# Moving row factors of a pooling stage from VectorE to GpSimd, and splitting its first residual pair by chunk

## The chip, the cores and the metric

The kernel runs on one NeuronCore of a Trainium2 chip. Its engines are named as the profile names them: PE is TensorE (PEld its weight loads), DVE is VectorE, ACT is ScalarE, POOL is GpSimd, and SP issues the transfers. The metric is the device time of one execution in microseconds (us); less is better.

## The reference

A stack of layers over 256 frames of 1024 channels. The stretch that matters is the hand-over from the first block to the second: a final norm, then a second norm, a pooling mixer with a residual sum, and the gated feed-forward stage after it.

```
h = h + ffn(...)                      # end of the first block (stage F1)
x = rms_norm(h, norm_final)
h = rmsnorm(x, mix_norm[0])
pooled_g = trailing mean of h over (2, 4, 8, 16) frames, group g of 256 channels
y = (pooled - h) @ pool_w[g] + pool_b
x = x + y * pool_scale                # stage POOL
x = x + conv_ffn_2(rmsnorm(x, ffn_norm[0]), ...)   # stage F2
```

## The kernel before

The activations lie transposed in SBUF: `xT` (inside the tensor `gx`) holds 8 chunks of 128 channels, each 128 partitions by 256 frames in float32. Each matmul runs on numbers that are split in a high part and a low part. ACT makes the high part (`split_x` in the scalar program, L1209, a copy with a gain into `xx`, which counts up the semaphore `s_xh`), and DVE the low part (`split_x` in the vector program, L1742, gain times `xT` less the high part, which counts up `s_xl`). The weights come as units that ACT and DVE split in the same way (L1206, L1737). Every engine runs a program written out by hand, in the order of the code, and the engines meet only at semaphores.

Stage POOL has four groups of 256 channels, two chunks each. PE multiplies the split chunks with the pool weights (L433 to L435) while the sums of squares of the last chunks come in. DVE makes the row factors from the sums: a chain of 12 tiny instructions (L2285 to L1777) gives `ra`, one number per frame. ACT scales the products with it into `zz` (L1644). DVE also multiplies `ra` into a diagonal, `dg` (L1812), PE spreads it over all partitions (L535, L536), and DVE copies that to `rb` (L1817), which counts up `s_rb`. PE then applies the averaging windows to `zz`, 16 pairs of short matmuls (L1172, L1174), and counts up `s_zw` for each group. ACT adds bias and scale to the results, `pu` (L1651, chunk by chunk, `average(k)`), and counts up `s_uu` after the second chunk of a group.

DVE has to bring `xT` through the final norm, `xT * norm_final * rb` (`normed`, L2298, one instruction for each of the 8 chunks), and then adds `pu` for each pair of chunks (`averages(g)`, L2305), which counts up `s_res`. ACT and DVE split the new chunks for stage F2, ACT squares them for the next norm (L1215, L1221), and DVE adds the squares up (L1750). In F2 PE takes the gate unit for chunks 0 and 1, then the value unit for chunks 0 and 1, and from chunk 2 on gate and value for one chunk after the other (L474, L476). Each chunk takes four pairs of matmuls of its own and waits for `s_xh` and `s_xl` of that chunk (`x_here`).

GpSimd has nothing to do up to the last attention stage, where it sets parts of the tiles `bm` (L2366, L2367). The sums that F2 needs for its own norm go through `fold_sums` and `low_sums` (L1793, L1798).

Of the kernel before, what the change touches and what calls it, by code (L numbers as in the profile page):

```python
# [10 lines left out]
ALU = mybir.AluOpType  # L11
# [3 lines left out]
S, D, KD = 256, 1024, 8  # L15
# [26 lines left out]
A, F0, B, F1, POOL, F2, DD, F3 = range(8)  # L42
# [59 lines left out]
def build(nc, dram, out):  # L102
    plan, first = unit_plan()
    N_UNITS = len(plan)
    with ExitStack() as ctx:
        def sb(name, shape, dt=F32, stack=ctx):
            return stack.enter_context(nc.sbuf_tensor(name, shape, dt))
# [5 lines left out]
        def sem(name):  # L113
            return ctx.enter_context(nc.semaphore(name))
# [5 lines left out]
        s_con, s_vec, s_win, s_bias, s_out, s_sin = (  # L120
            sem(f"s_{x}") for x in ("con", "vec", "win", "bias", "out", "sin"))
# [5 lines left out]
        s_xh, s_xl, s_res = sem("s_xh"), sem("s_xl"), sem("s_res")  # L127
# [3 lines left out]
        s_dg, s_row, s_rb, s_ones = sem("s_dg"), sem("s_row"), sem("s_rb"), sem("s_ones")  # L131
# [18 lines left out]
            sem(f"s_{x}") for x in ("kr", "krr", "krt", "qr", "rope", "qrt", "qre"))  # L150

        s_pp, s_zz, s_zw, s_gg, s_uu = (sem(f"s_{x}") for x in ("pp", "zz", "zw", "gg", "uu"))

        s_dv, s_ac = sem("s_dv"), sem("s_ac")

# [4 lines left out]
        xT = gx[:, KD:].rearrange("p (k s) -> p k s", k=KD)  # L160
# [52 lines left out]
        pu = sb("pu", [128, KD, S], F32, pool_mem)  # L213
# [11 lines left out]
        def vcol(name, i):  # L225
            return vec[:, VEC_AT[name] + i:VEC_AT[name] + i + 1]
# [11 lines left out]
        rbb = rb[:, :].unsqueeze(1).to_broadcast([128, 2, S])  # L238
# [5 lines left out]
        def bk(s, i):  # L244


            return bank[(2 * FLIP[s] + i) % 4]
# [56 lines left out]
        def n_x(s, k):  # L304

            return 8 * s + k + 1

        def n_res(s, c):

            return 4 * s + c + 1  # L310
# [7 lines left out]
        ROW = {F0: 1, F1: 2, POOL: 3, F2: 4, F3: 5}  # L318
# [872 lines left out]
        def scalar_program(e):  # L1191
# [16 lines left out]
            def split_x(s, k):  # L1208
                e.activation(xx[:, k, 0, :], xT[:, k, :], ACT.Copy, scale=gain_of(s, k)).then_inc(s_xh, 1)  # L1209
# [423 lines left out]
            def pool_mixer():  # L1633
                s = POOL
                u = first[s]
                e.wait_ge(s_rc, COL[s])
                for g in range(NG):
                    b = bk(s, g)
                    if g < 3:
                        e.wait_ge(s_pp, g + 1)  # L1640
                    else:
                        e.wait_ge(s_used, u + 1)
                    for h in range(2):
                        last = e.activation(zz[:, h, g * 256:(g + 1) * 256], b[:, h * 256:(h + 1) * 256], ACT.Copy,  # L1644
                                            scale=ra[:, 2 + h:3 + h])
                    last.then_inc(s_zz, 1)

                def average(k):
                    g, m = k // 2, k % 2
                    e.wait_ge(s_zw, g + 1)  # L1650
                    done = e.activation(pu[:, k, :], bk(s, g)[:, m * 256:(m + 1) * 256], ACT.Identity,  # L1651
                                        scale=vcol("pool_scale", k), bias=bs[:, k:k + 1])
                    if m == 1:
                        done.then_inc(s_uu, 1)

                def averages(g):
                    average(2 * g)
                    average(2 * g + 1)

                def split_pair(g):  # L1660
                    e.wait_ge(s_res, n_res(s, g))
                    split_x(F2, 2 * g)
                    split_x(F2, 2 * g + 1)

                averages(0)
                average(2)
                split_pair(0)
                average(3)
                squares(F2, 0)
                split_pair(1)  # L1670
                averages(2)
                squares(F2, 1)
                split_pair(2)
                averages(3)
                squares(F2, 2)
                split_pair(3)
                squares(F2, 3)
                high_sums(F2)
                hi(u + 5)
# [41 lines left out]
        def vector_program(e):  # L1721
# [7 lines left out]
            def after_own():  # L1729
                e.wait_ge(s_dv, own["n"])  # L1730
# [549 lines left out]
            def pool_mixer():  # L2280
                s = POOL
                u = first[s]
                e.wait_ge(s_sum, s + 1)
                sums = SB[:, 0, 0:4].rearrange("p (h w) -> p h w", h=2)
                e.tensor_scalar(va[:, 0:2], sums[:, :, 0], 1.0 / D, EPS, ALU.mult, ALU.add)  # L2285
                kept(e.tensor_scalar(va[:, 2:4], sums[:, :, 1], 1.0 / D, None, ALU.mult))
                after_own()
                kept(e.scalar_tensor_tensor(out=va[:, 2:4], in0=va[:, 0:2], scalar=EPS, in1=va[:, 2:4], op0=ALU.mult,
                                            op1=ALU.add))
                rsqrt(va, ra, ta).then_inc(s_rc, 1)  # L2290
                norm_diag(s, ra)
                norm_row(s, 0)
                e.wait_ge(s_rb, ROW[s])
                e.wait_ge(s_xh, n_x(s, KD - 1))

                def normed(*chunks):
                    for k in chunks:
                        kept(e.scalar_tensor_tensor(out=xT[:, k, :], in0=xT[:, k, :], scalar=vcol("norm_final", k),  # L2298
                                                    in1=rb[:, :], op0=ALU.mult, op1=ALU.mult))

                def averages(g):
                    xp = xT[:, 2 * g:2 * g + 2, :]
                    e.wait_ge(s_uu, g + 1)
                    after_own()
                    e.tensor_tensor(xp, xp, pu[:, 2 * g:2 * g + 2, :], ALU.add).then_inc(s_res, 1)  # L2305

                normed(0, 1, 2)
                averages(0)
                normed(3)
                split_x(F2, 0)  # L2310
                split_x(F2, 1)
                averages(1)
                normed(4, 5)
                split_x(F2, 2)
                split_x(F2, 3)
                normed(6, 7)
                averages(2)
                add_squares(F2, 1)
                split_x(F2, 4)
                split_x(F2, 5)  # L2320
                averages(3)
                add_squares(F2, 2)
                split_x(F2, 6)
                split_x(F2, 7)
                lo(u + 3)
                add_squares(F2, 3)
                fold_sums(F2)
                low_sums(F2)
                lo(u + 4)
# [31 lines left out]


        def gpsimd_program(e):
            e.wait_ge(s_used, first[DD])
            for b in bm:
                e.memset(b[0:64, :, 64:128], -1e30)  # L2366
                last = e.memset(b[0:64, :, 320:384], -1e30)  # L2367
            last.then_inc(s_bm, 1)
# [15 lines left out]
        @block.gpsimd  # L2384
        def _(e):
            gpsimd_program(e)
# [130 lines left out]
```

## Time and profile before

| what | value |
|---|---|
| median of 3 runs | 1062.54 us (1062.38 to 1062.83) |
| time of the profiled execution | 1062.58 us |
| its span in the trace | 1060.8 us |
| PE busy | 1056.1 us, 6764 matmuls |
| DVE busy | 835.5 us |
| ACT busy | 649.2 us |
| POOL busy | 1.3 us |
| granted PE clock in the stretch from 575 to 600 us | 1.00 (the 2.4 GHz level) |

The time of the profiled execution has 1.78 us beside its span. The span counts from the first to the last recorded event. Busy time of an engine is the time in which an instruction of it is on record; matmuls overlap, so PE starts the next one before the record of the last has ended, and the distance between starts is what PE needs for one. In a row of a timeline the first number is the start, the second how long it took, and xN says that N instructions are merged. Where an engine sat idle, the row ends with the idle time and what ended it.

### The profile page before, as it was taken

The page shows a single profiled execution, that of the slowest core. Times are in us where ns is not written, and L with a number is a line of the kernel's source. Part 1 is how long each engine was busy: PE and PEld are TensorE (multiplying, and loading weights), DVE is VectorE, ACT ScalarE, POOL GpSimd, SP SyncE. Part 2 cuts the span into 40 slices and gives each one's busy share as a digit, 9 for nine tenths or more (in the row PEclk, how much of TensorE's full clock was granted, in tenths as well). Part 3 has the DMA queues.
Part 4 walks back from the last instruction along what each step waited for, and adds up shares of the span by engine and source line. Part 5 has one row for each costly group of instructions (what it writes and reads, how often), then busy time and mean ns, then how long its engine had stood idle before and what let it go on. Part 6 is the DMA issues. An engine that isn't in the chain of part 4 may idle for free.

```text
span 1060.8 us, 16688 instructions
## 1 busy us (share of the span) xinstructions
PE 1056.1 (100%) x6764; PEld 941.3 (89%) x6764; DVE 835.5 (79%) x1329; ACT 649.2 (61%) x904; POOL 1.3 (0%) x8
## 2 busy tenths in 40 slices
PE   9999999999999999999999999999999999999998
PEld 8999888888898898888889888888988898888888
DVE  6896899786667789987667999876658768999851
ACT  7665587564367757765557577654557755766540
POOL 0000000000000000000000000000000000000000
PEclk9999999999999999999999999999999999999999
DMA  8554356555525165655652466565555533655540
GB/s 312 196 199 160 119 199 238 199 176 194 170 101 189 54 240 189 223 199 188 218 189 80 156 217 229 183 218 189 181 187 182 175 129 127 233 203 207 203 159 25
DMA packets 32237, 191.83 MB, mean 181 GB/s; under 512 B 4512, under 2 KB 6304, under 8 KB 12320
## 3 DMA queue, kind: packets, MB, share of 16 engines
q1 hardware_dynamic: 32016, 190.49, 51.2%
q8 instruction: 54, 0.88, 0.3%
q10 hardware_dynamic: 144, 0.26, 0.1%
q14 instruction: 23, 0.19, 0.1%
HBM read 189.69 MB, written 1.05 MB: 180 GB/s over the span
## 4 chain that ended last, share of the span: by engine, by line
PE 99%; DMA 0%; DVE 0%; ACT 0%; SPq 0%; issue 0%; DVEq 0%
PE banks L474 22%; PE TB L474 12%; PE SB L474 12%; PE banks L476 12%; PE TB L476 6%; PE SB L476 6%; PE banks L433 4%; PE banks L434 3%; PE banks L435 3%; PE banks L703 3%; PE banks L704 3%; PE banks L716 3%; PE banks L644 2%; PE banks L697 1%; PE banks L699 1%; PE banks L711 1%
## 5 line engine op out<-in xcount | busy, mean ns | idle before, releaser
L1737 DVE TENSOR_TENSOR wlo<-raw,whi 128x2048 fp32r<-128x2048 f32 (+2 forms) x180 | 395.8, 2202 | 77.3 <-ACT whi L1206 77.3
L1206 ACT ACTIVATE whi<-raw 128x2048 fp32r<-128x2048 f32 (+2 forms) x180 | 330.3, 1840 | 84.2 <-PE TB L476 24.7
L474 PE MATMUL banks<-xx,whi 128*128 128x512 f32 x752 | 262.1, 390 | 0.0
L476 PE MATMUL banks<-xx,wlo 128*128 128x256 f32 x752 | 212.2, 282 | 0.0
L474 PEld LDWEIGHTS banks<-xx,whi 128*128 128x128 f32 x752 | 141.2, 188 | 29.3
L476 PEld LDWEIGHTS banks<-xx,wlo 128*128 128x128 f32 x752 | 142.3, 189 | 0.0
L474 PE MATMUL TB<-xx,whi 128*128 128x512 f32 x336 | 117.8, 390 | 0.2 <-DVE xx L1742 0.2
L474 PE MATMUL SB<-xx,whi 128*128 128x512 f32 x320 | 111.8, 390 | 0.0
L476 PE MATMUL TB<-xx,wlo 128*128 128x256 f32 x336 | 94.8, 282 | 0.0
L474 PE MATMUL banks<-hx,whi 128*128 128x512 f32 x264 | 91.7, 390 | 0.0
L476 PE MATMUL SB<-xx,wlo 128*128 128x256 f32 x320 | 90.3, 282 | 0.0
L1291 ACT ACTIVATE ct<-gp,vec 128x256 f32<-128x256 f32 x88 | 48.3, 596 | 57.0 <-DVE gp L1913 57.0
L474 PEld LDWEIGHTS TB<-xx,whi 128*128 128x128 f32 x336 | 63.1, 188 | 13.4 <-issue 0.3
L476 PE MATMUL banks<-hx,wlo 128*128 128x256 f32 x264 | 74.5, 282 | 0.0
L474 PEld LDWEIGHTS SB<-xx,whi 128*128 128x128 f32 x320 | 60.1, 188 | 12.5
L476 PEld LDWEIGHTS TB<-xx,wlo 128*128 128x128 f32 x336 | 63.6, 189 | 0.0
L474 PE MATMUL TB<-hx,whi 128*128 128x512 f32 x176 | 61.2, 390 | 0.0
L474 PE MATMUL SB<-hx,whi 128*128 128x512 f32 x176 | 61.2, 390 | 0.0
L476 PEld LDWEIGHTS SB<-xx,wlo 128*128 128x128 f32 x320 | 60.6, 189 | 0.0
L474 PEld LDWEIGHTS banks<-hx,whi 128*128 128x128 f32 x264 | 49.6, 188 | 10.3
L703 PE MATMUL banks<-whi,xx 128*128 128x512 f32 x128 | 51.8, 404 | 0.0
L704 PE MATMUL banks<-whi,xx 128*128 128x512 f32 x128 | 50.6, 395 | 0.0
(272 smaller groups left out, 2027.5 us busy)
## 6 DMA issues: line engine op xcount, KB each, us to landing
raw<-in_gate SPq DMA_DIRECT2D x44, 1024.0 KB, 4.8
raw<-in_up SPq DMA_DIRECT2D x44, 1024.0 KB, 4.8
raw<-in_down SPq DMA_DIRECT2D x32, 1024.0 KB, 4.8
raw<-in_down SPq DMA_DIRECT2D x16, 768.0 KB, 4.4
raw<-in_d_kq SPq DMA_DIRECT2D x8, 1024.0 KB, 4.9
raw<-in_a_kq SPq DMA_DIRECT2D x6, 1024.0 KB, 5.7
raw<-in_a_o SPq DMA_DIRECT2D x4, 1024.0 KB, 5.6
raw<-in_b_o SPq DMA_DIRECT2D x4, 1024.0 KB, 4.8
```

The source lines that it names most:

```text
L433: e.matmul(po, ah, bh, start=start, stop=False, skip_group_check=True)
L434: e.matmul(po, ah, bl, start=False, stop=False, skip_group_check=True)
L435: return e.matmul(po, al, bh, start=False, stop=stop, skip_group_check=True)
L474: e.matmul(po[:, 0:512], wh[:, k, sl], a[:, kk, :, :].rearrange("p w s -> p (w s)"), start=start, stop=stop, skip_group_check=True)
L476: return e.matmul(po[:, 0:256], wl[:, k, sl], a[:, kk, 0, :], start=False, stop=stop, skip_group_check=True)
L644: last = e.matmul(b[o, q * 128:(q + 1) * 128], vv[:, h, col], pt[:, a, c * 128:(c + 1) * 128], start=(h == 0), stop=(c != 1), skip_group_c ...
L703: e.matmul(po, xx[:, k, 0, sl], wh[:, k % 4, :], start=k == 0, stop=False, skip_group_check=True)
L704: e.matmul(po, xx[:, k, 1, sl], wh[:, k % 4, :], start=False, stop=False, skip_group_check=True)
L716: return e.matmul(slot_bank(s, i, h)[:, :], xx[:, k, 0, sl], wl[:, k % 4, :], start=False, stop=k == KD - 1, skip_group_check=True)
L1206: e.activation(whi[n % RING][:, 0:nk * w], raw[n % RAW][:, 0:nk * w], ACT.Copy).then_inc(s_hi, 1)
L1291: e.activation(ct[:, m, :], g[:, m, 0:S], ACT.Identity, scale=cw(0, 2 * i + m), bias=cb(2 * i + m)).then_inc(s_tap, 1)
L1737: e.tensor_tensor(wlo[n % RING][:, 0:nk * w], raw[n % RAW][:, 0:nk * w], whi[n % RING][:, 0:nk * w].bitcast(F32), ALU.subtract).then_inc(s ...
```

## The change

Three things change. On DVE, chunks 0 and 1 are normed, and then `pu` is added to each alone: to chunk 0 once ACT has written `pu` of chunk 0 (a new semaphore `s_u0`), which counts up a new `s_c0`, and to chunk 1 after `s_uu`. On ACT, chunk 0 is split after `s_c0` and chunk 1 after `s_res`, and `pu` of chunks 2 and 3 comes behind the two splits, where chunk 2 stood ahead of them. The norm of chunks 2 to 7 goes to GpSimd: six products with `norm_final`, one chunk each, counted by `s_pv`, as soon as the first splits of stage POOL are done (`s_xh`, `s_xl`), and three products with `rb`, one pair of chunks each, counted by `s_pn`, once `rb` is there. DVE's `averages(g)` waits for `s_pn`. The instruction that GpSimd has ahead of its first product (ISA, below) stands ahead of all its waits, at the start of the program.

```diff
@@ scalar program, pool_mixer
-                    if m == 1:
+                    if k == 0:
+                        done.then_inc(s_u0, 1)
+                    elif m == 1:
                         done.then_inc(s_uu, 1)
...
                 averages(0)
-                average(2)
-                split_pair(0)
-                average(3)
+                e.wait_ge(s_c0, 1)
+                split_x(F2, 0)
+                e.wait_ge(s_res, n_res(s, 0))
+                split_x(F2, 1)
+                averages(1)
                 squares(F2, 0)
@@ vector program, pool_mixer
                 def averages(g):
                     xp = xT[:, 2 * g:2 * g + 2, :]
                     e.wait_ge(s_uu, g + 1)
-                    after_own()
+                    e.wait_ge(s_pn, g)
                     e.tensor_tensor(xp, xp, pu[:, 2 * g:2 * g + 2, :], ALU.add).then_inc(s_res, 1)

-                normed(0, 1, 2)
-                averages(0)
-                normed(3)
+                normed(0, 1)
+                after_own()
+                e.wait_ge(s_u0, 1)
+                e.tensor_tensor(xT[:, 0, :], xT[:, 0, :], pu[:, 0, :], ALU.add).then_inc(s_c0, 1)
+                e.wait_ge(s_uu, 1)
+                e.tensor_tensor(xT[:, 1, :], xT[:, 1, :], pu[:, 1, :], ALU.add).then_inc(s_res, 1)
+                e.wait_ge(s_c0, 1)
                 split_x(F2, 0)
                 split_x(F2, 1)
                 averages(1)
-                normed(4, 5)
                 split_x(F2, 2)
                 split_x(F2, 3)
-                normed(6, 7)
                 averages(2)
@@ gpsimd program
+            e.wait_ge(s_vec, 16)
+            e.wait_ge(s_xh, n_x(POOL, KD - 1))
+            e.wait_ge(s_xl, n_x(POOL, KD - 1))
+            for k in range(2, KD):
+                e.tensor_scalar(xT[:, k, :], xT[:, k, :], vcol("norm_final", k), None, ALU.mult).then_inc(s_pv, 1)
+            e.wait_ge(s_rb, ROW[POOL])
+            for c in range(1, 4):
+                xp = xT[:, 2 * c:2 * c + 2, :]
+                e.wait_ge(s_pv, 2 * c)
+                e.tensor_tensor(xp, xp, rbb, ALU.mult).then_inc(s_pn, 1)
             e.wait_ge(s_used, first[DD])
```

DVE before, from the copy to `rb` to the split of chunks 2 and 3 (line numbers of the kernel before):

```order
L1817 COPY rb<-TB 128x256 [waits s_row]
L2298 SCALAR_TENSOR_TENSOR gx<-gx,vec,rb 128x256 [waits s_xh,s_rb]
L2298 SCALAR_TENSOR_TENSOR gx<-gx,vec,rb 128x256 x2
L2305 TENSOR_TENSOR gx<-gx,pu 128x512 [waits s_dv,s_uu]
L2298 SCALAR_TENSOR_TENSOR gx<-gx,vec,rb 128x256
L1742 SCALAR_TENSOR_TENSOR xx<-gx,vec,xx 128x256 [waits s_xh] x2
L2305 TENSOR_TENSOR gx<-gx,pu 128x512 [waits s_dv,s_uu]
L2298 SCALAR_TENSOR_TENSOR gx<-gx,vec,rb 128x256 x2
L1742 SCALAR_TENSOR_TENSOR xx<-gx,vec,xx 128x256 [waits s_xh] x2
```

DVE in the changed kernel at the same place (its lines lie 5 further down, those of this function partly more):

```order
L1822 COPY rb<-TB 128x256 [waits s_row]
L2303 SCALAR_TENSOR_TENSOR gx<-gx,vec,rb 128x256 [waits s_xh,s_rb]
L2303 SCALAR_TENSOR_TENSOR gx<-gx,vec,rb 128x256
L2315 TENSOR_TENSOR gx<-gx,pu 128x256 [waits s_u0,s_dv]
L2317 TENSOR_TENSOR gx<-gx,pu 128x256 [waits s_uu]
L1747 SCALAR_TENSOR_TENSOR xx<-gx,vec,xx 128x256 [waits s_xh,s_c0]
L1747 SCALAR_TENSOR_TENSOR xx<-gx,vec,xx 128x256 [waits s_xh]
L2310 TENSOR_TENSOR gx<-gx,pu 128x512 [waits s_pn,s_uu]
L1747 SCALAR_TENSOR_TENSOR xx<-gx,vec,xx 128x256 [waits s_xh] x2
```

Three `normed` instructions (L2298) have left this piece, and the one add of 512 columns for the first pair has become two of 256, the first of them behind `s_u0` alone. Three more `normed` instructions leave DVE further on.

ACT before, from the first `pu` to the split of chunks 2 and 3:

```order
L1651 ACTIVATE pu<-banks,small,vec 128x256 [waits s_zw] x3
L1209 ACTIVATE xx<-gx,vec 128x256 [waits s_res]
L1209 ACTIVATE xx<-gx,vec 128x256
L1651 ACTIVATE pu<-banks,small,vec 128x256 [waits s_zw]
L1215 ACTIVATE ssum<-gx 128x512 [waits s_sum]
L1209 ACTIVATE xx<-gx,vec 128x256 [waits s_res]
L1209 ACTIVATE xx<-gx,vec 128x256
```

ACT in the changed kernel at the same place:

```order
L1652 ACTIVATE pu<-banks,small,vec 128x256 [waits s_zw] x2
L1210 ACTIVATE xx<-gx,vec 128x256 [waits s_c0]
L1210 ACTIVATE xx<-gx,vec 128x256 [waits s_res]
L1652 ACTIVATE pu<-banks,small,vec 128x256 [waits s_zw] x2
L1216 ACTIVATE ssum<-gx 128x512 [waits s_sum]
L1210 ACTIVATE xx<-gx,vec 128x256 [waits s_res]
L1210 ACTIVATE xx<-gx,vec 128x256
```

The third `pu` has moved from ahead of the first pair's splits to behind them, and each split of that pair has a wait of its own.

GpSimd in the changed kernel, up to its first memset:

```order
L2375 ISA
L2375 TENSOR_SCALAR gx<-gx,vec 128x256 [waits s_xl,s_xh,s_vec]
L2375 TENSOR_SCALAR gx<-gx,vec 128x256 x5
L2380 TENSOR_TENSOR gx<-gx,rb 128x512 [waits s_pv,s_rb]
L2380 TENSOR_TENSOR gx<-gx,rb 128x512 [waits s_pv] x2
L2383 MEMSET bm 64x4x64 [waits s_used]
```

Nine products are new there; before, the memset was its first instruction behind the start-up.

## Rows read from the trace of the kernel before

**Rows 1.** Page: engines' busy time, then the chain's shares by engine.

```profile
PE 1056.1 (100%) x6764; PEld 941.3 (89%) x6764; DVE 835.5 (79%) x1329; ACT 649.2 (61%) x904; POOL 1.3 (0%) x8
...
PE 99%; DMA 0%; DVE 0%; ACT 0%; SPq 0%; issue 0%; DVEq 0%
```

**Rows 2.** Waits of PE, whole span: who waited for whom, total, times, longest.

```profile
PE SB L682 <- DVE ones L2331: 1.1, 1, 1.1
PE TB L474 <- DVE xx L1742: 0.2, 1, 0.2
```

**Rows 3.** Timeline of PE from the spread of the row factors into F2.

```profile
574.82 0.38 PE L535 MATMUL TB<-dg,ones 128*128 128x128 f32 x2
...
575.26 0.41 PE L1172 MATMUL banks<-wins,zz 128*128 128x144 f32 x2
...
578.79 0.39 PE L1174 MATMUL banks<-wins,zz 128*128 128x128 f32 x2
579.35 0.47 PE L474 MATMUL TB<-xx,whi 128*128 128x512 f32 x1 [0.18 <-DVE xx L1742]
...
582.21 0.39 PE L474 MATMUL TB<-xx,whi 128*128 128x512 f32 x1
...
584.98 0.39 PE L474 MATMUL TB<-xx,whi 128*128 128x512 f32 x1
...
587.76 0.39 PE L474 MATMUL TB<-xx,whi 128*128 128x512 f32 x1
```

**Rows 4.** Chain of waits from 576.4 us: start, length, what.

```profile
576.40 1.03 ACT pu L1651 x2
...
577.45 0.70 DVE gx L2305
...
578.18 0.52 ACT xx L1209
...
578.72 0.50 DVE xx L1742
579.22 0.14 issue
```

**Rows 5.** Timeline of DVE, from 569 to 587 us.

```profile
569.02 0.43 DVE L1863 TENSOR_TENSOR gx<-rtmp,gx 128x256 f32<-128x256 f32 x1
570.33 0.48 DVE L1742 SCALAR_TENSOR_TENSOR xx<-gx,small,xx 128x256 fp32r<-128x256 f32 x1 [0.88 <-ACT xx L1209]
570.73 0.15 DVE L2285 TENSOR_SCALAR small<-SB 128x2 f32<-128x2 f32 x1
...
573.04 0.48 DVE L1812 TENSOR_SCALAR dg<-con,small 128x128 f32<-128x128 f32 x2
575.46 0.43 DVE L1817 COPY rb<-TB 128x256 f32<-128x256 f32 x1 [1.94 <-PE TB L536]
575.92 1.28 DVE L2298 SCALAR_TENSOR_TENSOR gx<-gx,vec,rb 128x256 f32<-128x256 f32 x3
...
584.02 0.89 DVE L1742 SCALAR_TENSOR_TENSOR xx<-gx,vec,xx 128x256 fp32r<-128x256 f32 x2
...
586.59 0.88 DVE L1742 SCALAR_TENSOR_TENSOR xx<-gx,vec,xx 128x256 fp32r<-128x256 f32 x2
```

**Rows 6.** Groups by line and shape, 572 to 588 us: busy, mean ns, idle before.

```profile
L1651 ACT ACTIVATE pu<-banks,small,vec 128x256 f32<-128x256 f32 x8 | 4.0, 554 | 0.4 <-PE banks L1174 0.4
...
L1209 ACT ACTIVATE xx<-gx,vec 128x256 fp32r<-128x256 f32 x8 | 3.6, 502 | 1.6 <-DVE gx L2305 1.6
...
L1750 DVE TENSOR_TENSOR ssum<-ssum,sq 128x512 f32<-128x512 f32 x2 | 1.4, 684 | 0.0
```

**Rows 7.** Timeline at 763 us: GpSimd's memsets and a DVE product beside them.

```profile
763.27 0.31 POOL L2367 MEMSET bm<- 64x256 f32 x1
...
763.52 0.30 POOL L2366 MEMSET bm<- 64x256 f32 x1
763.53 0.43 DVE L1863 TENSOR_TENSOR gx<-rtmp,gx 128x256 f32<-128x256 f32 x1
```

More of the change, by code:

```diff
@@ L152, in build @@
         s_pp, s_zz, s_zw, s_gg, s_uu = (sem(f"s_{x}") for x in ("pp", "zz", "zw", "gg", "uu"))
+        s_u0, s_c0, s_pv, s_pn = sem("s_u0"), sem("s_c0"), sem("s_pv"), sem("s_pn")
         s_dv, s_ac = sem("s_dv"), sem("s_ac")
```

## The prediction

> **What bounds the kernel now.** I read the page first: PE is busy for 1056.1 of 1060.8 us, and the chain that ended last is PE for 99% of the span [rows 1]. So only time that PE loses counts. The view of who waited for whom gives PE 1.1 us of waiting at the start of the program, and 0.2 us for a split of DVE on its way into TB [rows 2]; that second one is the place of this change, and the longest wait of PE after the start. PE's timeline shows it. The last pair of window matmuls (L1174) starts at 578.79, and two such pairs of short matmuls take 0.44 us from start to start (574.82 to 575.26), one 0.22, so PE is free for F2 at 579.01. F2's first matmul starts at 579.35, and is on record with 0.47 instead of the 0.39 us of the later ones [rows 3]. PE loses 0.34 us, and up to 0.08 more if the longer first matmul is a part of the stop: 0.42 us, which is all that this place can give back. The chain of waits says what it waited for: two `pu` on ACT from 576.40, DVE's add of the first pair at 577.45, ACT's split at 578.18, DVE's split at 578.72, and 0.14 us of issue [rows 4].
>
> After that PE has no stop in this stage. It reaches chunk 2 at 582.21, chunk 4 at 584.98 and chunk 6 at 587.76 [rows 3].
>
> **The first pair, if GpSimd disturbed nobody.** A `normed` on DVE is 0.40 us from start to start when several follow each other (1.28 for three, less the 0.08 by which a record of 0.48 is longer than its step) [rows 5]. Two of them after the copy end at about 576.75. ACT's first `pu` takes 0.55 [rows 6] from 576.40 [rows 4], so it is there at 576.96, and DVE has 0.2 us of slack before it. An add of 256 columns takes 0.43 (L1863) [rows 5], so chunk 0 is ready at 577.39. ACT ends its second `pu` at 577.43 [rows 4] and splits chunk 0 in 0.50 [rows 6], to 577.95. DVE adds chunk 1 meanwhile, 577.45 to 577.88, and splits chunk 0 in 0.48 [rows 5], to 578.46. With the same 0.14 of issue [rows 4], PE could start at 578.60, before it is free at 579.01. The stop goes: −0.42 us.
>
> Chunk 1 is split by ACT to 578.40 and by DVE to 578.87, and PE needs it 0.69 us after its start (a chunk of one unit takes a quarter of the 2.77 us from chunk 2 to chunk 4 [rows 3]). The `pu` of chunks 2 and 3 now stand behind these splits on ACT: 578.35 to about 579.40. PE waits for them too (`s_uu` at 2), but only 1.39 us after its start, at 580.40. That edit costs nothing; the two first chunks' gate matmuls cover it.
>
> **The later pairs.** From DVE's add of a pair (0.70 [rows 4]) over ACT's split (0.50) and DVE's split (0.48) to PE, with 0.05 between them and 0.14 of issue, are 1.87 us; for pairs 2 and 3 DVE has an add of squares of 0.68 [rows 6] in front of its split, which makes it 2.00. Without the stop PE wants chunks 2, 4 and 6 at 581.87, 584.64 and 587.42 (0.34 ahead of [rows 3]). So the adds may start no later than 580.0, 582.6 and 585.4. By ACT's order they can start at 579.4, 582.1 and 584.8, as the six `normed` that leave DVE there stood beside waits for `pu` anyway. Those 6 × 0.40 = 2.4 us of DVE are hidden work, and their removal gives PE nothing.
>
> **GpSimd's products.** No row of this trace has GpSimd read SBUF. Below, a product could be as quick as on DVE: 0.40 for one chunk (`normed`) [rows 5], 0.70 for a pair [rows 4]. Above, I take the memset, which writes 256 columns in 0.25 from start to start [rows 7], and count as many such steps as there are tiles read and written: 2 × 0.25 = 0.50 for one chunk, 3 × 2 × 0.25 = 1.50 for a pair. I take 0.45 and 1.1, the middle. The first six can start when DVE's split of chunk 7 is done, at 570.81 [rows 5], and end 2.7 us later, at 573.6; they are not needed before `rb`, at 575.89. The three pairs then end at 577.0, 578.1 and 579.2. The limits above leave 4.05, 3.3 and 3.15 us for each of them. Even at twice my upper bounds (1.0 and 3.0) they would end at about 580.0, 583.0 and 586.0 (the first six at 577.0), and PE would lose 0.6 us: with the stop gone that is +0.2. GpSimd as too slow an engine is not the danger. Only a page has a price: by the Trainium skill, "GPSIMD Engine Reference", section 3.1, a sum of two tiles of 2048 columns takes 4497 ns, so a quarter of it, about 1.12 us, is an estimate for a pair, with which the sum would stay as it is.
>
> **Two engines at one memory.** The unknown that decides is what DVE loses while GpSimd reads beside it. The trace has GpSimd write beside a DVE add with two inputs in SBUF: the add takes 0.43 at 763.53, under a memset [rows 7], as it does with GpSimd idle at 569.02 [rows 5]. It never has GpSimd read. From below, DVE loses nothing. From above, the two take turns, and each DVE instruction waits for GpSimd's whole product. By then GpSimd has three products ready, just as `rb` is there, and DVE has five instructions up to the first split. Let x be the delay of that split. The time changes by 578.60 + x − 579.35 us, but not by less than −0.42 (in the least case PE starts at 579.01). So up to x = 0.4 the whole gain stays, and from x = 0.75 on the kernel is slower than before. One product ahead gives x = 1.1 − 0.2 = 0.9 (the slack above): +0.15. Three give 3.1: +2.35. Between none and three I take the middle, one and a half: x = 1.45, **+0.7 us**. I do not take nothing, since in this place a read by each engine is asked for at the same moment, and nothing in the rows shows that they pass each other; nor all three, since DVE's second `normed` and the second add follow an instruction of their own without a wait, and may go ahead.
>
> The Trainium skill, "SBUF — State Buffer", section "Who interferes with whom", states that a DVE instruction with two SBUF inputs and a GpSimd instruction that reads SBUF exclude each other for the whole instruction, and that one that only writes does not disturb. On the write the trace agrees (0.43 and 0.43); no row of before shows the read. By it alone the sum would go to the upper end, +2.35, without it to −0.42; it speaks against this change.
>
> The same can hit the stretch before. The six first products run from 570.8 to 573.6, beside DVE's chain of tiny instructions (570.73 to 572.93) and the diagonal, which ends at 573.52 [rows 5]. PE takes the diagonal at 574.82 and `zz` at 575.26 [rows 3]; 1.15 us are left after issue. Most of the chain is waiting for its own results, so of 2.7 us I expect under 1.15, and cost it at nothing; with the cover gone it is at most 2.7 − 1.15 = +1.55.
>
> **Sum.** Against the profiled execution: 1062.58 − 0.42 (stop) + 1.12 (two engines) = 1063.28 us. The median of the runs is 0.04 below the profiled time, so 1063.2 us.
>
> **The rivals.**
> - GpSimd disturbs nobody, or no more than 0.4 us: −0.42, 1062.1 us. For it: the untouched add beside the memset. Against: that was a write. Chance 0.33.
> - Forecast, one or two turns in front of the first split: x from 0.9 to 2.0, +0.15 to +1.25. 1062.7 to 1063.8 us. Chance 0.40.
> - The slower side: all three products of GpSimd go ahead of DVE, each in turn, between the copy to `rb` and the first split. x = 3.1, +2.35, 1064.9 us; with products of 1.5 us it is +3.55. It counts as slower from x = 0.75, and can be told from no change from x = 2.9. Chance 0.16.
> - The tiny chain is held up until PE waits for the diagonal or `zz`: up to +1.55, with the forecast's turns behind it up to 1064.8 us. Against: 1.15 us of cover. Chance 0.07.
> - GpSimd's first product is slow to start, by some us beyond anything in the rows, so that the adds of later pairs wait: from 2 us of slowness on the first six products are late. Chance 0.03.
> - More DVE time in hand makes a later stage quicker: I see no wait of PE that it could end [rows 2]. Chance 0.01.
>
> **Range and chances.** From 1061.9 (the first case, less 0.2 for the spread of the runs) to 1065.0 (all three turns). What a measurement of this kernel can tell from no change is 0.2%, 2.1 us. Only the third case and the tails of the last ones pass it: faster 0.01, same 0.82, slower 0.17.
>
> **What would show it.** In the profile after: three GpSimd products of a pair from about 575.9, about 1.1 us each; the idle time of PE before F2's first matmul, 0.34 before, at 1.0 (0 if nothing is disturbed, 2.7 with three turns); DVE's `normed`, adds and first splits with longer records, or starts later than their semaphores, while GpSimd reads; and the add of the second pair no longer preceded by `normed`. The split of chunk 0 ending at 578.5 would show the forecast wrong by my term for two engines, and PE waiting for chunk 2, 4 or 6 that for GpSimd's speed. A PE wait before 575.26 would show that the tiny chain has lost its cover.

## The result and the profile after

The changed kernel takes 1064.61 us (median of 11 runs, 1064.16 to 1066.63) against 1062.54 us before (now 11 runs too, 1062.04 to 1063.19). The medians differ by 2.1 us, a ratio of 1.0019. The ratio of the comparison is 1.0023, with a 95% interval of 1.0015 to 1.0031; it is close to that of the means (1.0024), since five of the changed kernel's runs lie a good microsecond above the rest. It is slower by a small effect that the interval still tells from none. The profiled execution took 1064.56 us, with a span of 1062.8 us, where before it was 1062.58 and 1060.8.

The page's engine times and its shares of the chain, which answer to [rows 1]:

```profile
PE 1056.6 (99%) x6764; PEld 941.7 (89%) x6764; DVE 836.3 (79%) x1324; ACT 648.9 (61%) x904; POOL 11.0 (1%) x17
...
PE 97%; DVE 2%; ACT 1%; issue 1%; DVEq 0%; ACTq 0%
```

PE did the same work. GpSimd went from 1.3 to 11.0 us of busy time, and in the chain 2% has passed to DVE and 1% to ACT. The waits of PE, which answer to [rows 2]:

```profile
PE TB L475 <- DVE xx L1747: 2.0, 1, 2.0
```

The wait for DVE's split, 0.2 us before, is 2.0 us now. PE's timeline, from the first matmul of the sums in stage POOL to the spread of F2's sums, shows it in its place:

```profile
567.72 0.95 PE L1138 MATMUL SB<-ones,ssum 128*128 128x1 f32 x8
...
578.94 0.38 PE L1175 MATMUL banks<-wins,zz 128*128 128x128 f32 x2
581.33 0.47 PE L475 MATMUL TB<-xx,whi 128*128 128x512 f32 x1 [2.00 <-DVE xx L1747]
...
594.58 0.28 PE L530 MATMUL SB<-sx,ones_r 128*128 128x256 f32 x1
```

The windows end at 578.94 + 0.22 = 579.16, F2 starts at 581.33: a stop of 2.17 us, 0.34 before [rows 3]. From the sums' first matmul to the spread PE took 26.86 us; in the trace of before the same two stand at 567.56 and 592.61, 25.05 us. The difference of 1.81 us is that of the two stops (1.83). I use this stretch below, since the start of the program varies from run to run: the profiled executions reach the sums' first matmul between 567.06 and 568.38 us, in kernels that are alike up to there (PE's wait for a weight split at 8 us is one reason: 0.16 us before, 0.70 to 0.86 in three of the kernels below). The next stretch, from F2's spread to F3's, is 292.82 us before and 292.83 after.

DVE's timeline, which answers to [rows 5], and GpSimd's beside it:

```profile
571.34 0.34 DVE L1766 TENSOR_SCALAR small<-small 128x4 int32<-128x4 int32 x1
...
572.33 0.26 DVE L1774 SCALAR_TENSOR_TENSOR small<-small 128x4 f32<-128x4 f32 x1
...
573.61 0.48 DVE L1817 TENSOR_SCALAR dg<-con,small 128x128 f32<-128x128 f32 x2
575.62 0.42 DVE L1822 COPY rb<-TB 128x256 f32<-128x256 f32 x1 [1.53 <-PE TB L537]
576.08 0.88 DVE L2303 SCALAR_TENSOR_TENSOR gx<-gx,vec,rb 128x256 f32<-128x256 f32 x2
577.22 1.15 DVE L2315 TENSOR_TENSOR gx<-gx,pu 128x256 f32<-128x256 f32 x1 [0.26 <-ACT pu L1652]
578.30 1.48 DVE L2317 TENSOR_TENSOR gx<-gx,pu 128x256 f32<-128x256 f32 x1
579.71 1.88 DVE L1747 SCALAR_TENSOR_TENSOR xx<-gx,vec,xx 128x256 fp32r<-128x256 f32 x2
581.50 0.68 DVE L2310 TENSOR_TENSOR gx<-gx,pu 128x512 f32<-128x512 f32 x1
```

```profile
571.18 5.50 POOL L2375 TENSOR_SCALAR gx<-gx,vec 128x256 f32<-128x256 f32 x6 [570.75 <-DVE xx L1747]
576.65 4.25 POOL L2380 TENSOR_TENSOR gx<-gx,rb 128x512 f32<-128x512 f32 x3
```

GpSimd's six products of one chunk took 5.50 us, 0.92 each, and the three of a pair 4.25 us, 1.42 each from start to start. They thus ended at about 578.07, 579.48 and 580.90. DVE's two adds of 256 columns, 0.43 each elsewhere, are on record with 1.15 and 1.48, and ended at 578.37 and 579.78. Its first split ended at 581.19, as the chain shows:

```profile
577.22 1.15 DVE gx L2315
578.37 0.60 DVE gx L2317
578.98 0.73 issue
579.71 1.49 DVE xx L1747
581.19 0.14 issue
```

Each of the three DVE instructions ended some 0.3 us behind one of GpSimd's products (whose single ends are worked out from the mean): one DVE instruction between two products, twice, and the third behind the last product. The pair behind these is quick again (0.68 at 581.50), as GpSimd is done. And the two norm products at 576.08 took 0.88 together, as before, although GpSimd's sixth product of one chunk ran up to 576.68.

### The profile page after: what moved, and what is told of

Same layout as the page of the kernel before. It is cut to its first block, busy times and chain, and to the rows that moved or that the text cites. A ratio compares the mean times of both kernels' runs of the same rounds, so it can differ in the third digit from the quotient of the medians.

```text
span 1062.8 us, 16697 instructions
## 1 busy us (share of the span) xinstructions
PE 1056.6 (99%) x6764; PEld 941.7 (89%) x6764; DVE 836.3 (79%) x1324; ACT 648.9 (61%) x904; POOL 11.0 (1%) x17
## 4 chain that ended last, share of the span: by engine, by line
PE 97%; DVE 2%; ACT 1%; issue 1%; DVEq 0%; ACTq 0%
PE banks L475 21%; PE TB L475 12%; PE SB L475 12%; PE banks L477 11%; PE TB L477 6%; PE SB L477 6%; PE banks L434 3%; PE banks L436 3%; PE banks L435 3%; PE banks L704 3%; PE banks L717 3%; PE banks L705 3%; PE banks L645 2%; PE banks L698 1%; PE banks L700 1%; PE banks L712 1%
```

## The experiments

All kernels are compared by their median, the two stretches of the profiled execution, and the stops of PE in the stage. "To F2" is from the sums' first matmul to F2's spread, "to F3" from there to F3's spread; the clock column says in how many runs the mean granted clock was 0.998 in place of 1.0. The ratio of each experiment is to runs of the kernel before on the same chip, whose medians lie between 1062.57 and 1062.82 us.

| kernel | median, us | ratio, interval | to F2, us | to F3, us | low clock |
|---|---|---|---|---|---|
| before | 1062.54 | | 25.05 | 292.82 | none |
| changed | 1064.61 | 1.0023, 1.0015 to 1.0031 | 26.86 | 292.83 | 5 of 11 |
| changed, again | 1065.50 | 1.0025, 1.0014 to 1.0036 | 26.86 | 292.83 | 4 of 7 |
| chunks only | 1062.95 | 1.0005, 0.9996 to 1.0014 | 25.15 | 293.04 | 0 of 11 |
| reads elsewhere | 1065.57 | 1.0028, 1.0017 to 1.0039 | 27.55 | 293.07 | 2 of 7 |
| writes elsewhere | 1064.41 | 1.0015, 1.0006 to 1.0024 | 26.77 | 293.07 | 0 of 10 |
| filled stop | 1064.73 | 1.0021, 1.0012 to 1.0030 | 26.90 | 292.82 | 0 of 11 |
| two products held | 1063.91 | 1.0009, 1.0000 to 1.0018 | 26.24 | 292.83 | 0 of 10 |
| all three held | 1064.45 | 1.0019, 1.0010 to 1.0028 | 28.33 | 292.83 | 4 of 10 |
| products only | 1064.03 | 1.0011, 1.0002 to 1.0020 | 26.48 | 292.82 | 0 of 10 |
| chunks before norms | 1062.74 | 1.0000, 0.9991 to 1.0009 | 24.76 | 293.06 | 0 of 11 |
| stop without GpSimd | 1064.49 | 1.0017, 1.0009 to 1.0026 | 26.63 | 292.83 | 0 of 11 |
| single products only | 1062.65 | 1.0000, 0.9991 to 1.0009 | 24.62 | 293.14 | 0 of 11 |
| fewer squares | 1062.06 | 0.9995, 0.9986 to 1.0004 | 24.62 | 292.83 | 0 of 11 |

### Chunks only

Against the changed kernel; `...` stands for lines left out:

```diff
                     e.wait_ge(s_uu, g + 1)
-                    e.wait_ge(s_pn, g)
+                    after_own()
...
                 split_x(F2, 0)
                 split_x(F2, 1)
+                normed(2, 3)
                 averages(1)
+                normed(4, 5)
                 split_x(F2, 2)
                 split_x(F2, 3)
+                normed(6, 7)
...
-            (GpSimd's nine products and their waits)
```

> The first pair added and split chunk by chunk, as in the change, but all eight norm products on DVE, none on GpSimd. Theory (GpSimd's reads hold up DVE's): DVE's adds of 256 columns take 0.43 us again, PE's stop of 2.0 us before F2 is gone, 1062.1 us, 0.4 under the kernel before. Rival (the new order and its semaphores are what is late): the stop stays at 1 us or more, 1063.5 or above.

The adds on DVE's timeline:

```profile
577.89 0.43 DVE L2315 TENSOR_TENSOR gx<-gx,pu 128x256 f32<-128x256 f32 x1 [0.26 <-ACT pu L1652]
578.27 0.43 DVE L2317 TENSOR_TENSOR gx<-gx,pu 128x256 f32<-128x256 f32 x1
```

and PE's last windows and first matmul of F2:

```profile
579.61 0.38 PE L1175 MATMUL banks<-wins,zz 128*128 128x128 f32 x2
579.75 0.48 PE L475 MATMUL TB<-xx,whi 128*128 128x512 f32 x1
```

The adds take 0.43 again, and PE has no stop before F2. So the new order and its semaphores are not what is late. But the gain is not there either: the norm products of chunks 2 and 3 now stand behind the first splits, DVE comes late to chunks 2, 3 and 4, and the stretch is 25.15 us, the time 1062.95 where 1062.1 was expected. The theory holds for the stop and fails for the time.

### Reads elsewhere, and writes elsewhere

```diff
 chunks only, and on GpSimd, reads (DVE waits for s_pn only behind its last split of F2's chunks):
+            for k in range(6):
+                e.tensor_scalar(idle[:, k, 0:256], con[:, 0:256], vcol("norm_final", k), None, ALU.mult)
+            e.wait_ge(s_rb, ROW[POOL])
+            for c in range(1, 4):
+                e.tensor_tensor(idle[:, 5 + c, :], con[:, 0:512], con[:, 256:768], ALU.mult).then_inc(s_pn, 1)
 or, writes:
+            for k in range(19):
+                if k == 11:
+                    e.wait_ge(s_rb, ROW[POOL])
+                if k > 8:
+                    e.wait_ge(s_pn, k - 8)
+                e.memset(idle[:, k % 9, :], 0.0).then_inc(s_pn, 1)
```

> As the chunks-only kernel, and beside it GpSimd runs six products of 256 columns and three of 512 at the same two places, but reads a constant tile and writes a scratch tile that nobody reads. Theory (turns at the read): DVE's adds and splits from 577 to 581 are stretched as in the change (1.15, 1.48 us) and PE's stop is 1.5 to 2.3 us, 1064.0 to 1065.5. Rival (the change is slow since DVE or ACT waits for GpSimd's results): nothing waits here, so as the chunks-only kernel, 1062.1.

> As the chunks-only kernel, and GpSimd fills a scratch tile of 512 columns 19 times over the same stretch, which writes SBUF and reads nothing. Theory (only reads collide): no DVE instruction is stretched, 1062.1. Rival (any work of GpSimd at SBUF holds DVE up): stretched adds and a stop as in the change, above 1063.5.

With the reads elsewhere, DVE's timeline is that of the changed kernel, almost to the hundredth:

```profile
577.35 1.15 DVE L2316 TENSOR_TENSOR gx<-gx,pu 128x256 f32<-128x256 f32 x1 [0.26 <-ACT pu L1653]
578.42 1.49 DVE L2318 TENSOR_TENSOR gx<-gx,pu 128x256 f32<-128x256 f32 x1
579.83 1.88 DVE L1748 SCALAR_TENSOR_TENSOR xx<-gx,vec,xx 128x256 fp32r<-128x256 f32 x2
```

Nothing in this kernel waits for GpSimd in the stretch shown, and the tiles that GpSimd touches are not those of DVE. The 1.15 and 1.49 us are thus neither waits for data nor for a semaphore: DVE's instructions of two SBUF tiles and GpSimd's products of two tiles exclude each other, whichever tiles they are. The stop before F2 is 2.0 us again. The stretch of 27.55 us is 0.69 longer than the changed kernel's; DVE's own norm products behind the splits, which make chunks only 0.53 longer than single products only, can be most of that. The median, 1065.57, lies just above the 1065.5 that I gave.

With the writes, the adds of DVE, with two inputs in SBUF, are untouched. But something else is not:

```profile
570.49 5.19 POOL L2385 MEMSET idle<- 128x512 f32 x11 [570.04 <-DVE xx L1748]
577.12 3.76 POOL L2385 MEMSET idle<- 128x512 f32 x8 [1.44 <-DVE rb L1823]
```

```profile
573.01 2.82 DVE L1818 TENSOR_SCALAR dg<-con,small 128x128 f32<-128x128 f32 x2
...
578.24 0.42 DVE L2316 TENSOR_TENSOR gx<-gx,pu 128x256 f32<-128x256 f32 x1 [0.26 <-ACT pu L1653]
578.62 0.43 DVE L2318 TENSOR_TENSOR gx<-gx,pu 128x256 f32<-128x256 f32 x1
```

The two products of the diagonal (one input in SBUF, one number per partition, 128 columns) take 2.82 us in place of 0.48 [rows 5], and PE waits 1.4 us for them. They end at 575.83, 0.15 us behind the whole first train of memsets (575.68): here DVE got no turn between two of GpSimd's instructions, though five memsets began after it. So neither expectation for this kernel came true as a whole: writes leave the adds alone, as the theory said, but a dense train of them holds up another kind of DVE instruction, ahead of the adds, and that makes the stretch 26.77 us where chunks only has 25.15. In the changed kernel, where GpSimd is in its six products of one chunk at that place, the diagonal took its usual 0.48.

The Trainium skill, "SBUF — State Buffer", section "Who interferes with whom", has both: a DVE instruction with two SBUF inputs contends with a GpSimd instruction that reads SBUF, and a DVE instruction in a 2-port mode, which a `tensor_scalar` can enter, contends with GpSimd. The runs agree, with 1.15 and 1.48 for 0.43, and 2.82 for 0.48; that the diagonal ran in such a mode no run shows. Of that mode it also says that the first to issue keeps the shared pair for its whole instruction. The three ends 0.3 us behind GpSimd's products of a pair fit a lock of that kind. Three measurements do not fit, and there the measurement decides: the norm products (0.88 for two, as before, of which one and a half ran beside a GpSimd product of one chunk), the diagonal (0.48, as before) beside such products, and the diagonal that five later memsets went ahead of. GpSimd's products of one tile read SBUF too, so that it reads is not the whole condition; whether the second input or the kind of instruction makes the difference was not tested.

### Products only, two products held, all three held

```diff
 products only: the changed kernel, but ACT in the order of before for the first pair, and DVE (five lines out)
+                averages(0)
 two products held (c == 2), or all three (c == 1): GpSimd
                 e.wait_ge(s_pv, 2 * c)
+                if c == 2:
+                    e.wait_ge(s_xl, n_x(F2, 1))
```

> One part of the change alone: GpSimd's nine products, while DVE adds the first pair in one instruction of 512 columns and ACT keeps the order of before. Theory (turns): DVE has three instructions between its norm products and the first split in place of four, so at most two turns fall in front of it: PE's stop is 1.3 to 1.7 us, 1063.6 to 1064.2. Rival (splitting the pair is innocent, and all GpSimd time counts): a stop of 2.0 to 2.5 as in the change, 1064.5 or more.

> The changed kernel, with GpSimd's second and third product of a pair held back until DVE has made the first two splits for F2. Theory (each of GpSimd's products, 1.4 us, holds up one DVE instruction): one turn is left ahead of the first split, PE's first stop is about 0.4 us in place of 2.0; the second product then holds up DVE's add of chunks 2 and 3, and PE stops again at chunk 2 by about 1 us; the stretch from the sums' first matmul to F2's spread is 26.5 us (25.05 before, 26.86 changed), the time 1063.5 to 1064.3. Rival (the delay is one fixed cost of having GpSimd in the stage): the first stop stays at 2.0.

> The changed kernel, with all three products of a pair held back until DVE has made the first two splits for F2. Theory: no stop of PE ahead of F2 and adds of 0.43 us, but chunks 2 and 3 come late, by the product of 1.4 us and one turn: a stop of 1.0 to 1.7 us at chunk 2, 1063.3 to 1064.0. Rival (the six products of one chunk do the harm, not the three of a pair): the stop ahead of F2 stays.

With products only, the add of the first pair (512 columns) waits out the first product, the first split the second, and the second split the third:

```profile
577.84 0.98 DVE L2306 TENSOR_TENSOR gx<-gx,pu 128x512 f32<-128x512 f32 x1 [0.70 <-DVE gx L2299]
579.41 2.26 DVE L1743 SCALAR_TENSOR_TENSOR xx<-gx,vec,xx 128x256 fp32r<-128x256 f32 x2 [0.58 <-ACT xx L1210]
```

PE's wait before F2 is 0.9 us on record, 1.0 from the end of the windows; a second, of 0.5, follows for chunk 1. That is under the 1.3 to 1.7 that I gave: with one add less, only two turns fall ahead of the first split, and they overlap ACT's splits.

With two products held, the first add is 1.16 long and the second 0.41: one turn, as there is one product. The held ones then catch the add of chunks 2 and 3, on record with 1.64 for 0.69:

```profile
577.38 1.16 DVE L2315 TENSOR_TENSOR gx<-gx,pu 128x256 f32<-128x256 f32 x1 [0.26 <-ACT pu L1652]
578.47 0.41 DVE L2317 TENSOR_TENSOR gx<-gx,pu 128x256 f32<-128x256 f32 x1
...
580.42 1.64 DVE L2310 TENSOR_TENSOR gx<-gx,pu 128x512 f32<-128x512 f32 x1 [0.35 <-ACT pu L1652]
```

PE stops for 0.5 us before F2 (from the end of the windows) and for 0.8 us at chunk 2, a stretch of 26.24 against 26.5 forecast. The harm goes with the number of products in front of the instruction, not with GpSimd's presence. With all three held there is no stop before F2, but one of 1.9 us at chunk 2, longer than the 1.0 to 1.7 expected: GpSimd's product is waited for, and then the add waits out the next. GpSimd's three products of a pair in this kernel (shortest, median and longest, in ns):

```profile
L2382 POOL TENSOR_TENSOR gx<-gx,rb x3: 1284/1292/1719, 578.8 to 581.3; 128x512 f32<-128x512 f32 x3
```

The first two ran without being held up, 1.28 and 1.29 us; the last one, which starts at 581.3, is 1.72 long, as DVE's add of 512 columns has its turn then. So the turns cost GpSimd too, and the 1.42 us of the changed kernel hold some 0.13 us of waiting for DVE. The stretch of 28.33 us also holds what a lower clock cost in this execution, 1.5 us (below).

### Filled stop, the changed kernel again, and a stop without GpSimd

The 11 runs of the changed kernel fall in two groups, 6 from 1064.16 to 1064.61 at a granted clock of 1.0, and 5 from 1065.62 to 1066.63 at 0.998.

```diff
 filled stop: PE, ahead of the gate unit of F2
+                    for _ in range(18):
+                        e.matmul(SB[:, 1, 0:128], ones_r[:, :], ones_r[:, :], start=True, stop=True,
+                                 skip_group_check=True)
 stop without GpSimd: chunks before norms (below), and on DVE ahead of the first split
+                for i in range(2):
+                    e.tensor_tensor(idle[:, i, :], con[:, :], con[:, :], ALU.mult)
```

> The changed kernel, with 18 matmuls of ones into an unused half of a PSUM tile between the windows and F2, some 2 us of PE work that fits into the stop. The runs of the changed kernel fall in two groups, 1064.2 to 1064.6 at a clock of 1.0 and 1065.6 to 1066.6 at 0.998. Theory (the idle PE gets a lower clock for a while, in some runs): all runs at 1.0, 1064.2 to 1064.6. Rival (the two groups have nothing to do with the stop): both groups appear again.

> The changed kernel once more, on one chip with the next kernel. Theory (a stop of 2 us lowers PE's clock in some runs): two groups again, near 1064.4 at clock 1.0 and 1.2 to 2.0 us above it at 0.998, with some 3 to 6 of the runs in the upper one. Rival (the groups were of one chip or one hour): a single group.

> No product on GpSimd: the kernel with chunks before norms, and ahead of the first split for F2 two DVE products of 896 columns on a constant tile, into a scratch tile that nobody reads, some 2.0 us. Theory (it is the stop of PE that matters, whoever makes it): PE stops for about 1.9 to 2.1 us, and the runs show both groups, one at clock 1.0 near 1064.4 and some at 0.998 above 1065.4. Rival (the lower clock comes from GpSimd and DVE working at once): all runs at 1.0, near 1064.4.

With the stop filled, none of 11 runs is at 0.998. The highest is 1065.26, still under the upper group, though seven of the 11 lie above the 1064.6 that I gave, for a reason that stays open. On another chip the changed kernel as it stands has both groups again (3 runs from 1064.46 to 1064.74, 4 from 1065.50 to 1065.97). The profile of the kernel with all three held was one of the low ones. Its windows (us, PE busy, granted clock, DMA share, GB/s) and its matmuls:

```profile
582.00:584.00 2.00, 0.52 (x3) 1.00 0.00 0
584.00:586.00 2.00, 2.00 (x10) 0.70 0.00 0
586.00:588.00 2.00, 2.00 (x7) 0.50 0.00 0
588.00:590.00 2.00, 2.00 (x12) 0.95 0.00 0
```

```profile
583.48 0.47 PE L475 MATMUL TB<-xx,whi 128*128 128x512 f32 x1 [1.89 <-DVE xx L1747]
...
585.72 0.63 PE L475 MATMUL TB<-xx,whi 128*128 128x512 f32 x1
...
586.36 0.63 PE L475 MATMUL banks<-xx,whi 128*128 128x512 f32 x1
```

After an idle time of 1.89 us PE runs on at 1.00 for somewhat more than a microsecond, then at 0.50, the 1.2 GHz level, for some 3.4 us, and then at 1.00 again. A pair of matmuls takes 0.64 us there in place of 0.35; the six pairs from 584.61 to 588.25 take 3.64 us in place of 2.1, 1.5 more. The two groups of the changed kernel lie 1.4 us apart (medians of 1064.43 and 1065.86). In reads elsewhere the lower clock left no such mark: its two runs at 0.998 (1065.57 and 1065.59) lie among the five at 1.0 (1065.27 to 1065.66). Why is not shown.

The stop without GpSimd was 1.8 us on record, a little shorter than the 2.0 of the changed kernel, and all 11 runs, on the same chip as the changed kernel's 7, were at 1.0. That is what my rival forecast, and not my theory. So a stop is needed for the lower clock (filled, it is gone), but that any stop will do is not shown: whether the shorter stop or the missing GpSimd made the difference stays open.

### Chunks before norms, single products only, fewer squares

```diff
 chunks before norms: no GpSimd, DVE
-                normed(0, 1)
+                normed(0, 1, 2)
                 (adds of chunks 0 and 1)
+                normed(3)
                 e.wait_ge(s_c0, 1)
 single products only: GpSimd keeps the six, DVE's averages(g) for g > 0, ahead of its wait for s_uu
+                    e.wait_ge(s_pv, 2 * g)
+                    kept(e.tensor_tensor(xp, xp, rbb, ALU.mult))
+                    after_own()
 fewer squares: single products only, and in F2's add_squares for c > 1, which leaves out most of the squares
+                at = slice(0, 4)
```

> No product on GpSimd; the first pair by chunk, with DVE's norm product of chunk 2 ahead of the two adds and that of chunk 3 between the adds and the first split, where DVE waits for ACT. Theory (what is left of the change without GpSimd gains the old stop): PE has no stop before F2 and none at chunk 2, the stretch from the sums' first matmul to F2's spread is 24.6 us against 25.05 before, 1062.1 us. Rival (as in the chunks-only kernel, DVE's throughput takes it back): a stretch of 25.0 or more, no gain.

> The changed kernel with GpSimd's six early products of one chunk kept, and the three products of a pair back on DVE, each just ahead of its add. Theory (only the products after the copy to rb are in DVE's way): no stop of PE before F2, DVE's tiny chain 0.5 us longer and hidden, the stretch from the sums' first matmul to F2's spread 24.6 to 24.8 us (25.05 before), 1062.1 to 1062.4. Rival (the six early ones cost as well): a PE stop at the diagonal, or a first split that is late, and 1063 or more.

> The kernel with single products only, but DVE adds up just 4 of each 256 columns of the squares of pairs 2 and 3, in place of all (0.68 us each). Left out: most of the squares of chunks 4 to 7 in the norm of F2, with nothing else changed. Theory (the 0.42 us won before F2 is mostly given back at 602 us, where PE now waits 0.3 to 0.4 us for DVE's low weights of F2's fifth unit): DVE's split of those weights comes about 1 us earlier, PE has no wait there, the stretch from F2's spread to F3's spread is 292.8 us as in the kernel before and not 293.1, and the time is 1062.1 to 1062.4. Rival (the give-back is elsewhere, or the gain is not there at all): 293.1 and 1062.6 again.

The first two reach what I took for the ceiling or come near it: no stop before F2, and 24.76 and 24.62 us to F2, 0.29 and 0.43 less than before. Their medians (1062.74 and 1062.65) are those of the kernel before on the same chips (1062.75 and 1062.63), all the same. The stretch to F3 takes it back, 293.06 and 293.14 for 292.82; both stretches together are 317.82 and 317.76 us for 317.87. Followed matmul by matmul, the difference arises at one place, where F2's third gate unit begins; in single products only:

```profile
601.82 0.28 PE L477 MATMUL SB<-xx,wlo 128*128 128x256 f32 x1
602.14 0.50 PE L475 MATMUL TB<-xx,whi 128*128 128x512 f32 x1
```

```profile
PEld TB L475 <- DVE wlo L1742: 0.4, 1, 0.4
```

```profile
577.55 0.43 DVE L2317 TENSOR_TENSOR gx<-gx,pu 128x256 f32<-128x256 f32 x1 [0.27 <-ACT pu L1652]
577.93 0.42 DVE L2319 TENSOR_TENSOR gx<-gx,pu 128x256 f32<-128x256 f32 x1
...
599.80 2.29 DVE L1742 TENSOR_TENSOR wlo<-raw,whi 128x2048 fp32r<-128x2048 f32 x1
```

The last of these is DVE's split of that unit's weights, which ends at 602.09, when PE has been waiting since about 601.94; the matmul at 602.14 is also followed by its next after 0.34 us in place of 0.23. In the kernel before, DVE's split (599.40, 2.29 long) ended at 601.69 and PE began at 601.88, without a stop; with the 0.05 us from DVE's end to PE's start that the changed one shows, that is 0.14 us of slack. PE had 0.42 us to win before F2, and DVE, which between 579 and 602 us has hardly a gap, allows little more than 0.1 of it. With fewer squares DVE gets to that split earlier:

```profile
598.26 2.29 DVE L1742 TENSOR_TENSOR wlo<-raw,whi 128x2048 fp32r<-128x2048 f32 x1
```

This kernel leaves out most of the squares of chunks 4 to 7, so it is no rival of the kernel before but shows where the gain went. The wait is gone, the stretch to F3 is 292.83, that to F2 still 24.62, together 317.45 and so 0.42 under before, and the median is 1062.06, 0.5 under the kernel before by its own median and 0.8 by that of the same chip (1062.82). The interval, 0.9986 to 1.0004, holds 1; the stretches, not the medians, bear this. None of the kernels that compute all of the reference beats the kernel before by what can be measured.

## Why the prediction was right, and where it was not

The median, 1064.61 us, lies in the stated range (1061.9 to 1065.0). The change of 2.07 us is just at the 2.1 us that I gave as what can be told from none, and the interval does tell it from none, so "no change" came true only barely. The median doesn't lie in the forecast's own part of it (1062.7 to 1063.8, chance 0.40), but above it, 0.3 us from the rival with all three of GpSimd's products in front (1064.9, chance 0.16). That rival's mechanism is what happened; its sum was near by luck, as shown below.

**The bound and the place.** Right. The whole difference of the profiled executions is made of PE's stop ahead of F2 (1.81 us) and of the start of the program (0.16); no other stage changed.

**The first pair undisturbed.** The chain was right to 0.2 us: in single products only, PE starts F2 without a stop, and DVE's adds and first split lie as I placed them (the split ends at 579.10, where `rb` is 0.48 later than before, against 578.46). The 0.42 us were right for another reason than mine. Without a stop F2's first matmul starts 0.14 us behind the last pair of windows, not 0.22, and is on record with 0.48 all the same (chunks only), so the longer record is no part of the stop: 0.56 − 0.14 = 0.42.

**"Two engines at one memory", +1.12 us.** The mechanism was the one forecast, the size was half of what it is. The stop grew by 1.81 where the term and the gain together gave +0.70, so the term measured 1.81 + 0.42 = 2.23 us. In the prediction's terms x is 581.33 − 0.15 − 578.60 = 2.58 against 1.45, with 0.15 for the program's later arrival. I took one and a half turns since DVE's second add "may go ahead" behind its first. It doesn't: the add that follows another without a wait had to give way too, and the rival with all three products ahead is what happened. But its sum (x = 3.1) was wrong in itself. It adds three whole products to DVE's path, while they run beside what DVE and ACT do and wait for anyway. The first split ended 0.29 us behind the last product, so what counts is when that ends: 576.65 + 4.25 + 0.29 = 581.19, against 578.61 undisturbed (578.46 with the 0.15), 2.58. By my own placing the last product ended at 579.2, which would give 579.2 + 0.29 − 578.46 = 1.0 for three turns (an estimate from these rows, if the split is again the one that waits for the last). The rest came from the length of the products (4.25 for 3.3, so 0.95) and from their start: the first began at 576.65, 0.6 us behind `rb`, since GpSimd was still at its own six (0.61). That 3.1 and 2.58 lie so close is luck.

**GpSimd's own speed.** A pair took 1.42 us, within my 0.70 to 1.50, and 1.28 to 1.29 where DVE didn't hold it up (all three held). A product of one chunk took 0.92, nearly twice my upper bound of 0.50, which was the step of a memset times the tiles touched. DVE's norm products didn't wait for the six, so this looks harmless, but the six ended at 576.68, 0.6 us behind `rb`, and put the three products of a pair that much later, on the adds and the first split. The estimate from the figure of the Trainium skill, "GPSIMD Engine Reference", section 3.1, 1.12 us for a pair, was low too.

**The tiny chain.** Right. It was 0.42 us late (diagonal at 573.61, with the program 0.15 later than before) and the cover of 1.15 us held. Five of its instructions are longer than before, the longest by 0.17.

**The later pairs cost nothing.** Right; chunk 2 begins 2.85 us behind F2's first matmul, 2.86 before [rows 3].

**The ceiling.** Wrong in a way that the result alone wouldn't have shown: I took the 0.42 us as a gain that the whole program keeps. DVE's weights at 602 us leave little more than 0.1 of it. What failed is the step from "all that this place can give back" to the sum, where "the stop goes: −0.42 us" stands as if nothing behind it set a limit. The sum lacked the slack of PE at the next places where it could wait for DVE.

**What was missing altogether.** That the stop of PE can lower its clock. In 5 of 11 runs it did, and the median of 1064.61 is the highest of the lower group. In the runs at 1.0 the change costs 1.9 us (1064.43 as their median).

## What to carry over

Before work is moved to GpSimd, look at what DVE does at the same moment: instructions with two SBUF inputs took turns with GpSimd's products of two tiles, whole instruction by whole instruction, and a short DVE instruction on the path (0.43 us) then took up to a whole product of GpSimd's (1.48). For such turns, ask when GpSimd's last product in front ends; adding the products up counts what they run beside. Put GpSimd's part where DVE waits or where its instructions have cover, as the six early products had, which made the tiny chain 0.42 us later and PE no later. And before a gain at one wait is booked, look at how much slack the same engine has at the following ones.

## What I had not expected of the hardware

- GpSimd multiplied 256 columns by one number per partition in 0.92 us, and 512 by a second tile in 1.28 to 1.29; DVE did the latter in 0.69 (single products only).
- GpSimd's memsets, which read nothing, stretched two DVE products of one SBUF input from 0.48 to 2.82 us, up to the end of the train, and DVE adds of two inputs not at all (0.42 and 0.43).
- Beside GpSimd's products of one tile and a number per partition, DVE's instructions lost at most 0.17 us each; beside its products of two tiles, up to a whole product.
- With all three held, PE ran at 0.50 of its clock for some 3.4 us, starting some 1.3 us behind the end of an idle time of 1.89. Stops of 1.9 to 2.0 us led to a mean clock of 0.998 in some runs only, and 18 matmuls of ones in the gap kept it at 1.0 in all 11.
